# Two blocks in fp32 on one core: new places for the expert stage's inner values, the scatter and the modulation chunks

## Chip, cores, metric

One NeuronCore of a Trainium2 chip runs the whole program in one launch. The metric is the device time of that launch in microseconds (us), lower is better.

## What is computed

x is 256 tokens by 1024 features, everything in fp32. A first block of two layers (windowed attention and MLP, then an RG-LRU block and MLP), then a second block: three mixers side by side, and a mixture of experts. The parts around the change are:

```python
def sq_relu_mlp(h, w1, w2):                      # D_FF = 4096
    return jnp.square(jax.nn.relu(h @ w1)) @ w2

def ada_modulation_2(cond, w, b):                # once for c, once for c_ctx
    return jnp.split(jax.nn.silu(cond) @ w + b, N_MOD, axis=-1)

hx = modulate(rmsnorm(x, norm1_g[layer]), mod_x[0], mod_x[1])
hc = modulate(rmsnorm(ctx, norm1_g[layer]), mod_c[0], mod_c[1])

for e in range(N_EXPERTS):                       # 16 experts, each token belongs to one group of 4
    he = (jax.nn.silu(h @ w_gate[e]) * (h @ w_up[e])) @ w_down[e]
    out = out + combine[:, e:e + 1] * he.astype(jnp.float32)
x = x + mod_x[5] * ff_x.reshape(B, L, D)
return rmsnorm(x, final_norm_g)
```

## The kernel before

**Stream of pieces.** All weights come in pieces of 128 partitions x 1024 fp32 (512 KB) through a ring of six buffers (RING, in load_program, lines 350 to 381). SyncE issues the DMA of a piece when the one six places earlier in the stream has been used up. A "w" piece is a weight for TensorE. An "a" piece is a modulation chunk's half: VectorE multiplies it with a condition vector and sums along the row (modulation, L1307), which gives a column of the modulation table MOD.

**Split of a weight.** TensorE multiplies fp32 as three products of rounded halves (mm3). ScalarE writes a piece's high part w_high (high_upto, L911), VectorE subtracts it and writes the low part w_low (low_upto, L1299). Both have four slots, so ScalarE may write the high part of a piece only when TensorE is through with the piece four places earlier (the wait on `used`). VectorE waits for w_high, TensorE for w_low. Every engine executes its list in order; VectorE's instructions are all issued through one helper, so the profile gives them line L347, and nearly all matmuls line L388: one goes by tile names.

**Second MLP of the first block** (W_MLP1, turns 8 to 15; mlp at L517, L995 and L1476). A turn handles 512 hidden features with eight w pieces, four for the first product (X0 to X3) and four for the second (S4 to S7), of 24 matmuls each. On VectorE the splits of a turn are those of S4 to S7, called L4 to L7 here, and those of the next turn's X0 to X3, L8 to L11. Between them stand the inner values (r_two, the square, and h_low, its low part, for halves a = 0 and 1) and two chunks of modulation, of two pieces each. The first 8 chunks of ada_w_2 are "double": each piece is multiplied with two condition vectors (c and c_ctx), which is two instructions on the tile junk instead of one. Before, turns 8 to 11 take the 8 double chunks and turns 12 to 15 take 8 single ones. Between turn 11 and turn 12 the context ctx is normalised and modulated (rms_rows, modulate_norm), and its low part is made.

**Experts** (L827 to L900 on TensorE, L1214 to L1247 on ScalarE, L1869 to L1910 on VectorE). The 256 tokens are sorted by group into tiles of 128 slots. Experts 0 to 3 work on two tiles, experts 4 to 15 on one. The order of pieces in the stream (MOE_SEQ, L78) for step p is: the gate pieces of expert p+1 (G0 to G3), the down pieces of expert p (D0 to D3), and the up pieces of expert p+1 (U0 to U3). For one tile each piece is six matmuls of 128x512. In step p TensorE does

```python
        if p < NE - 1:
            gate(p + 1, 0, 1)
        turn(p)
        if p < NE - 1:
            gate(p + 1, 1, 4)
        down(p)
        if p < NE - 1:
            up(p + 1)
        if p % 4 == 3:
            scatter(p // 4)
```

where turn(p) is four transposes of the expert's hidden values he (L856). The inner values of an expert are: ScalarE's sigmoid of the gate product (signs, tile sge), VectorE's product of the two (gates, tile sge), VectorE's he = sge * weight * up product (products, L1874, which waits for U3 of that expert), TensorE's transposes, ScalarE's high part (he_high) and VectorE's low part (turned, he_low). VectorE has the twelve splits of step p, called L0 to L11 (L0 is G0's, L4 is D0's, L8 is U0's). Before, the list reads: L0 to L3, products(p), L4, turned(p), L5 to L7, gates(p+1), L8 to L11.

**Results.** After four experts, the sum of a group lies in PSUM. ScalarE copies it out (results, L1224, tile y_experts). TensorE multiplies it with a 0/1 matrix that puts the rows back to their tokens (scatter, L873), in four rounds r through two banks, and VectorE adds each round to x with the modulation factor (results, L1884, add_branch). TensorE's round r waits for VectorE's additions of round r-2.

Of the kernel before, what the change touches and what calls it, by code (L numbers as in the profile page):

```python
# [26 lines left out]
D, S, P = 1024, 256, 128  # L27
# [43 lines left out]

ADA_COL = [2 * j for j in range(48)] + [96 + 2 * j for j in range(24)]

# [67 lines left out]
def y_at(i):  # L141

    return 0 if i == 0 else i % 2
# [239 lines left out]
def tensor_program(nc, m, s, arrived):  # L383
# [455 lines left out]
    def gate(p, first, last):  # L839
        if first == 0 and p > 0:  # L840
            pe.wait_ge(s.silu, tiles_upto(p - 1))
        for n in range(first, last):
            hidden(p, "g", n)

    def up(p):
# [26 lines left out]

    def scatter(i):  # L873

        tiles = tiles_of(4 * i)
        pe.wait_ge(s.y_out, i + 2)
        for r in range(4):
            if r >= 2 or i > 0:
                pe.wait_ge(s.x_add, X_MOE + 8 * i + 2 * (r - 2) + 2)
            for d in (2 * r, 2 * r + 1):  # L880
                for a, tile in enumerate(tiles):
                    ins = mm(PS[:, 1 + 2 * (r % 2), (d % 2) * 256:(d % 2 + 1) * 256], m.YE[:, y_at(i) + a, d * P:(d + 1) * P], m.SCAT[:, tile, :], a == 0, a == len(tiles) - 1)
            ins.then_inc(s.sc_mm, 1)

# [3 lines left out]
    for p in range(NE):  # L888
# [5 lines that stand above are left out]
        down(p)  # L894
        if p < NE - 1:
            up(p + 1)
        if p % 4 == 3:
            scatter(p // 4)
    square_sums(SQ_END, m.MEAN, m.T2, KT)


def scalar_program(nc, m, s, arrived, cvec, par, rpar, xT, tab, ident_d, gw, ctxT, posT, tab2, fpar, moe_tab):
# [175 lines left out]
    act.wait_ge(s.in_late, 48)  # L1078
    rms_rows(m.CTX, KT, m.T2, D, 4, None)
    modulated(MOD_CTX, 1)  # L1080
    mlp(W_MLP1 + 32, 12, 4)
    layer_norm(3)
# [154 lines left out]
    for p in range(NE):  # L1237
        w = MOE_AT.get((p + 1, "g", 0), W_END)
        high_upto(w + 5)
        turned(p)  # L1240
        if p < NE - 1:
            high_upto(w + 8)
            signs(p + 1)
            high_upto(w + 12)
        if p % 4 == 3:
            results(p // 4)
    rms_rows(m.X, KT, m.T2, D, 10, (s.x_add, X_MOE + 26, 2), m.MEAN)  # L1247

# [44 lines left out]
def vector_program(nc, m, s, arrived):  # L1293
# [12 lines left out]

    def modulation(junk, conds=((0, 0),), only=range(2)):  # L1307

        for j in only:
            c = ADA_AT[2 * ada[0] + j]  # L1310
            vv.wait_ge(arrived[c % RING], 16 * (c // RING + 1))
            for n, (v, off) in enumerate(conds):
                col = ADA_COL[ada[0]] + off + j
                op(vv.tensor_tensor_reduce, junk, m.piece(c), m.CB[:, v, :], 1.0, 0.0, ALU.mult, ALU.add, m.MOD[:, col:col + 1],
                   inc=s.ada if n == len(conds) - 1 else None)
        ada[0] += 1

# [157 lines left out]

    def mlp(w0, t0, turns, conds=((0, 0),)):  # L1476
        for i in range(turns):
            t, w = t0 + i, w0 + 8 * i
            low_upto(w + 5)
            for a in range(2):  # L1480
                vv.wait_ge(s.relu, 2 * t + a + 1)
                if t >= 1:
                    vv.wait_ge(s.h_high, 2 * t + a - 1)
                op(vv.tensor_tensor, m.R2[:, a, :], m.R1[:, a, :], m.R1[:, a, :], ALU.mult, inc=s.relu2)
                vv.wait_ge(s.h_high, 2 * t + a + 1)
                op(vv.tensor_tensor, m.H1[1][:, a, :], m.R2[:, a, :], m.H1[0][:, a, :].bitcast(F32), ALU.subtract, inc=s.h_low)
                if a == 0:
                    low_upto(w + 6)
                    modulation(m.junk_mlp, conds)
                    low_upto(w + 7)  # L1490
            low_upto(w + 8)
            modulation(m.junk_mlp, conds)
            low_upto(w + 12)
# [63 lines left out]
    vv.wait_ge(s.silu_cc, 1)  # L1557
    mlp(W_MLP1, 8, 4, ((1, 0), (0, 48)))
    vv.wait_ge(s.in_late, 48)
    bias(144, 16, "ada_b2", 0)  # L1560
    rms_rows(4, m.CTX, m.CTX)
    lows = modulate_norm(MOD_CTX, m.CTX, "n1g", 144, 152, 1)
    lows()
    mlp(W_MLP1 + 32, 12, 4, ((1, 0),))
    op(vv.tensor_scalar, m.gate1, m.MOD[:, 88:96], 1.0, None, ALU.add)
# [317 lines left out]

    def results(i):  # L1884
        for r in range(4):
            vv.wait_ge(s.sc_mm, 4 * i + r + 1)
            for d in (2 * r, 2 * r + 1):
                add_branch(d, PS[:, 1 + 2 * (r % 2), (d % 2) * 256:(d % 2 + 1) * 256], m.MOD[:, 136 + d:137 + d])

# [7 lines left out]
    for p in range(NE):  # L1897
        w = MOE_AT.get((p + 1, "g", 0), W_END)
        if p > 0:
            low_upto(w + 4)  # L1900
            products(p)
            if p % 4 == 0:
                results(p // 4 - 1)
        low_upto(w + 5)
        turned(p)
        if p < NE - 1:
            low_upto(w + 8)
            gates(p + 1)
            low_upto(w + 12)
    results(3)  # L1910
    rms_rows(10, m.X[:, :, :], m.T1[:, :, :])
# [174 lines left out]
```

## Time and profile before

| | us |
|---|---|
| Median of 3 runs | 1676.21 (1666.42 to 1679.6) |
| Profiled execution, its own time | 1678.0 |
| Its span, first to last instruction | 1676.7 |
| TensorE (PE) busy | 1376.2 (82%) |
| VectorE (DVE) busy | 1159.0 (69%) |
| ScalarE (ACT) busy | 719.8 (43%) |
| Mean DMA rate over the span | 186 GB/s |

Times in a row of the trace are in us from the span's start. In a timeline row the bracket says how long the engine had been idle before the row, and what ended that. "PE" is TensorE's matmuls, whose ends are modelled, so that neighbouring matmuls overlap in the rows: the pace is the distance of their starts. PEclk in a table of windows is the granted TensorE clock, as a share of full speed.

### The profile page before, as it was taken

What the parts mean: (1) busy time and instruction counts of PE and PEld (TensorE: products, weight loads), DVE (VectorE), ACT (ScalarE), POOL (GpSimd) and SP (SyncE); (2) the same over time, 40 slices, a digit from 0 to 9 for tenths busy, and PEclk for the clock granted to TensorE, in tenths of its full rate; (3) what the DMA queues carried; (4) which work ended last, traced back from release to release, by engine and by line L of the source; (5) the groups of instructions that cost most, each with busy time, mean ns of one, the idle gap of its engine ahead of it and who ended that gap; (6) DMA issues with size and microseconds to landing.
All of it is one profiled execution on the core that took longest, in us unless ns stands there. A gap on an engine that the chain in (4) does not pass through costs nothing.

```text
span 1676.7 us, 20860 instructions
## 1 busy us (share of the span) xinstructions
PE 1376.2 (82%) x7808; PEld 1200.5 (72%) x7808; DVE 1159.0 (69%) x1541; ACT 719.8 (43%) x896; POOL 63.1 (4%) x54
## 2 busy tenths in 40 slices
PE   0862799997999977888985998655789999888885
PEld 0752799996777756888974797544777777777674
DVE  6657677776577567788766656985465557777775
ACT  2332335442565663334432333111244445666663
POOL 1100010000000001000000000430000000000000
PEclk9985999999999988999987998886889999999998
DMA  8425487874566445665760463100054556878782
GB/s 350 151 75 213 151 258 277 286 260 145 201 235 219 163 145 210 227 218 184 273 217 20 144 208 126 39 0 10 1 204 146 179 178 220 298 263 299 269 300 77
DMA packets 84069, 311.90 MB, mean 186 GB/s; under 512 B 9344, under 2 KB 9568, under 8 KB 83360
## 3 DMA queue, kind: packets, MB, share of 16 engines
q1 hardware_dynamic: 82080, 298.88, 51.1%
q10 hardware_dynamic: 1888, 11.69, 2.1%
q8 instruction: 61, 1.00, 0.2%
q14 instruction: 40, 0.33, 0.1%
HBM read 309.48 MB, written 1.05 MB: 185 GB/s over the span
## 4 chain that ended last, share of the span: by engine, by line
PE 61%; DVE 29%; ACT 6%; issue 2%; DMA 2%; DVEq 0%; POOL 0%; ACTq 0%; SPq 0%; POOLq 0%
PE ps L388 60%; DVE w_low L347 10%; DVE junk L347 5%; ACT w_high L347 2%; DVE t_one L347 1%; DVE t_two L347 1%; DVE rs L347 1%; DVE he L347 1%; DVE qp L347 1%; DMA ring<-stream 1%; DVE x L347 1%; PE ps L856 1%; DMA ring<-moe 1%; DVE sc L347 1%; DVE pf L347 1%
## 5 line engine op out<-in xcount | busy, mean ns | idle before, releaser
L347 DVE TENSOR_TENSOR w_low<-ring,w_high 128x1024 fp32r<-128x1024 f32 x376 | 461.6, 1228 | 196.2 <-ACT w_high L347 170.4
L347 ACT ACTIVATE w_high<-ring 128x1024 fp32r<-128x1024 f32 x376 | 398.9, 1061 | 327.1 <-PE ps L388 276.3
L388 PE MATMUL ps<-x_high,w_high 128*128 128x256 f32 (+1 forms) x784 | 235.8, 301 | 79.2 <-DVE x_low L347 71.6
L388 PE MATMUL ps<-x_low,w_high 128*128 128x256 f32 (+1 forms) x784 | 233.0, 297 | 0.0
L388 PE MATMUL ps<-x_high,w_low 128*128 128x256 f32 (+1 forms) x784 | 232.7, 297 | 0.0
L388 PEld LDWEIGHTS ps<-x_high,w_high 128*128 128x128 f32 x784 | 154.5, 197 | 90.5 <-issue 84.2
L347 DVE CUSTOM_DVE_ANT_0 junk<-ring,cond 128x1024 f32<-128x1024 f32 x133 | 165.3, 1243 | 20.9 <-DMA ring<-stream 3.6
L388 PE MATMUL ps<-h_high,w_high 128*128 128x256 f32 x512 | 147.7, 289 | 10.9 <-DVE h_low L347 10.9
L388 PEld LDWEIGHTS ps<-x_high,w_low 128*128 128x128 f32 x784 | 154.5, 197 | 2.8
L388 PEld LDWEIGHTS ps<-x_low,w_high 128*128 128x128 f32 x784 | 154.7, 197 | 2.5
L388 PE MATMUL ps<-h_low,w_high 128*128 128x256 f32 x512 | 146.9, 287 | 0.0
L388 PE MATMUL ps<-h_high,w_low 128*128 128x256 f32 x512 | 146.9, 287 | 0.0
L388 PE MATMUL ps<-w_high,xg_high 128*128 128x512 f32 x320 | 133.4, 417 | 0.0
L388 PE MATMUL ps<-w_low,xg_high 128*128 128x512 f32 x320 | 129.5, 405 | 0.0
L388 PE MATMUL ps<-w_high,xg_low 128*128 128x512 f32 x320 | 128.6, 402 | 0.0
L388 PE MATMUL ps<-x_whole,ring 128*96 128x256 f32 x512 | 114.8, 383 | 5.9 <-DVE x_whole L347 5.9
L388 PEld LDWEIGHTS ps<-h_high,w_high 128*128 128x128 f32 x512 | 100.4, 196 | 12.1 <-DVE h_low L347 12.1
L388 PEld LDWEIGHTS ps<-x_whole,ring 128*96 128x96 f32 x512 | 84.4, 165 | 33.9 <-issue 6.2
L388 PEld LDWEIGHTS ps<-h_low,w_high 128*128 128x128 f32 x512 | 100.6, 196 | 0.0
L388 PEld LDWEIGHTS ps<-h_high,w_low 128*128 128x128 f32 x512 | 100.4, 196 | 0.0
L388 PEld LDWEIGHTS ps<-w_high,xg_low 128*128 128x128 f32 x320 | 63.2, 198 | 14.0
L388 PEld LDWEIGHTS ps<-w_high,xg_high 128*128 128x128 f32 x320 | 63.7, 199 | 13.2
(299 smaller groups left out, 2170.3 us busy)
## 6 DMA issues: line engine op xcount, KB each, us to landing
ring<-stream SPq DMA_DIRECT2D x376, 512.0 KB, 4.6
ring<-moe SPq DMA_DIRECT2D x192, 512.0 KB, 4.6
tab_two<-tab ACTq DMA_DIRECT2D x1, 2824.0 KB, 14.1
gw<-gw ACTq DMA_DIRECT2D x1, 2304.0 KB, 13.3
cond<-cvec ACTq DMA_DIRECT2D x3, 512.0 KB, 6.8
x<-xT ACTq DMA_DIRECT2D x1, 1024.0 KB, 12.0
ctx<-ctxT ACTq DMA_DIRECT2D x1, 1024.0 KB, 4.8
pos<-posT ACTq DMA_DIRECT2D x1, 1024.0 KB, 6.9
```

Source lines behind the costliest of these rows:

```text
L347: return op(*a, **k).then_inc(self.sem, 1)
L388: return pe.matmul(out, stationary, moving, start=start, stop=stop, skip_group_check=True)
L856: ins = pe.transpose(PS[:, 2 + a, k * P:(k + 1) * P], m.HE[:, a, k * P:(k + 1) * P], m.ident)
```

## The change

Three parts. (1) In the second expert loop, for p >= 4, products(p) and turned(p) are moved ahead of splits: VectorE does L0, products, L1, L2, turned, L3 to L5, gates, L6 to L11, and ScalarE's copies are placed to match. ScalarE's copy of a group's results (y_experts) now stands ahead of the last two high parts of its step, where it stood behind them. (2) The scatter of a group is no longer one block after up(p+1); its four rounds follow the four gate pieces of expert 5, 9 and 13, and VectorE's additions stand one round at a time between L2 and gates. The last group's scatter stays at the end. (3) The chunks of ada_w_2 are reordered so that double and single ones alternate (A2_ORDER), one piece of a turn's first chunk is moved behind h_low of a = 1, and the context's modulation is moved from behind turn 11 to behind turn 14. Its normalisation stays behind turn 11.

```diff
+A2_ORDER = [0, 8, 1, 9, 2, 10, 3, 11, 4, 12, 5, 13, 6, 7] + list(range(14, 24))
+ADA_COL = [2 * j for j in range(48)] + [96 + 2 * j for j in A2_ORDER]
@@ TensorE
         for n in range(first, last):
             hidden(p, "g", n)
+            if p >= 5 and p % 4 == 1:
+                scatter(p // 4 - 1, n)
@@
-    def scatter(i):
+    def scatter(i, r):
@@
-        if p % 4 == 3:
-            scatter(p // 4)
+    for r in range(4):
+        scatter(3, r)
@@ ScalarE
     rms_rows(m.CTX, KT, m.T2, D, 4, None)
+    mlp(W_MLP1 + 32, 12, 3)
     modulated(MOD_CTX, 1)
-    mlp(W_MLP1 + 32, 12, 4)
+    mlp(W_MLP1 + 56, 15, 1)
@@
-        high_upto(w + 5)
+        high_upto(w + (5 if p < 4 else 3))
         turned(p)
         if p < NE - 1:
-            high_upto(w + 8)
+            high_upto(w + (8 if p < 4 else 6))
             signs(p + 1)
-            high_upto(w + 12)
+            high_upto(w + 10)
         if p % 4 == 3:
             results(p // 4)
+        if p < 4:
+            high_upto(w + 12)
@@ VectorE, MLP
+    def conditions():
+
+        col = ADA_COL[ada[0]]
+        if col < 96:
+            return ((0, 0),)
+        return ((1, 0), (0, 48)) if col < 112 else ((1, 0),)
...
                 if a == 0:
                     low_upto(w + 6)
-                    modulation(m.junk_mlp, conds)
+                    modulation(m.junk_mlp, conditions(), (0,), False)
                     low_upto(w + 7)
+            modulation(m.junk_mlp, conditions(), (1,))
             low_upto(w + 8)
-            modulation(m.junk_mlp, conds)
+            modulation(m.junk_mlp, conditions())
             low_upto(w + 12)
@@
-    mlp(W_MLP1, 8, 4, ((1, 0), (0, 48)))
+    mlp(W_MLP1, 8, 4)
     vv.wait_ge(s.in_late, 48)
+    rms_rows(4, m.CTX, m.CTX)
+    mlp(W_MLP1 + 32, 12, 3)
     bias(144, 16, "ada_b2", 0)
-    rms_rows(4, m.CTX, m.CTX)
     lows = modulate_norm(MOD_CTX, m.CTX, "n1g", 144, 152, 1)
     lows()
-    mlp(W_MLP1 + 32, 12, 4, ((1, 0),))
+    mlp(W_MLP1 + 56, 15, 1)
@@ VectorE, experts
         if p > 0:
-            low_upto(w + 4)
+            low_upto(w + (4 if p < 4 else 1))
             products(p)
-            if p % 4 == 0:
-                results(p // 4 - 1)
-        low_upto(w + 5)
+        low_upto(w + (5 if p < 4 else 3))
         turned(p)
         if p < NE - 1:
-            low_upto(w + 8)
+            for r in range(4):
+                low_upto(w + 3 + r)
+                if p >= 4 and p % 4 == 0:
+                    results(p // 4 - 1, r)
+            if p < 4:
+                low_upto(w + 8)
             gates(p + 1)
-            low_upto(w + 12)
-    results(3)
+            if p < 4:
+                low_upto(w + 12)
+    for r in range(4):
+        results(3, r)
```

Place one: VectorE in the one-tile experts, steps without results, before. sge is gates, he is products, he_low is turned.

```order
L347 TENSOR_TENSOR sge_1024_148<-sge_1024_148,ps 128x512
L347 TENSOR_TENSOR w_low<-ring_6144_49,w_high 128x1024 x8
L347 SCALAR_TENSOR_TENSOR he_1024_149<-sge_1024_148,rout_1024_146,ps 128x512
L347 TENSOR_TENSOR w_low<-ring_6144_49,w_high 128x1024
L347 TENSOR_TENSOR he_low<-ps,he_high 128x512
L347 TENSOR_TENSOR w_low<-ring_6144_49,w_high 128x1024 x3
```

The same place of the change (the helper's line is now L349):

```order
L349 TENSOR_TENSOR sge_1024_148<-sge_1024_148,ps 128x512
L349 TENSOR_TENSOR w_low<-ring_6144_49,w_high 128x1024 x7
L349 SCALAR_TENSOR_TENSOR he_1024_149<-sge_1024_148,rout_1024_146,ps 128x512
L349 TENSOR_TENSOR w_low<-ring_6144_49,w_high 128x1024 x2
L349 TENSOR_TENSOR he_low<-ps,he_high 128x512
L349 TENSOR_TENSOR w_low<-ring_6144_49,w_high 128x1024 x3
```

The eight splits between gates and products were L8 to L11 and the next step's L0 to L3. Now they are seven, L6 to L11 and the next L0: gates stands two splits earlier, products three.

Place two: TensorE around the first scatter, before. y_experts and scat are the scatter, ident and he the transposes of expert 4.

```order
L388 MATMUL ps<-w_high,xg_low 128x512
L388 MATMUL ps<-scat_1280_145,y_experts_2048_153 128x256 x16
L388 MATMUL ps<-w_high,xg_high 128x512
L388 MATMUL ps<-w_low,xg_high 128x512
L388 MATMUL ps<-w_high,xg_low 128x512
L388 MATMUL ps<-w_high,xg_high 128x512
L388 MATMUL ps<-w_low,xg_high 128x512
L388 MATMUL ps<-w_high,xg_low 128x512
L856 MATMUL ps<-ident_128_59,he_1024_149 128x128 x4
```

The same place of the change:

```order
L390 MATMUL ps<-w_high,xg_low 128x512
L390 MATMUL ps<-scat_1280_145,y_experts_2048_153 128x256 x4
L860 MATMUL ps<-ident_128_59,he_1024_149 128x128 x4
L390 MATMUL ps<-w_high,xg_high 128x512
L390 MATMUL ps<-w_low,xg_high 128x512
L390 MATMUL ps<-w_high,xg_low 128x512
L390 MATMUL ps<-w_high,xg_high 128x512
L390 MATMUL ps<-w_low,xg_high 128x512
L390 MATMUL ps<-w_high,xg_low 128x512
L390 MATMUL ps<-scat_1280_145,y_experts_2048_153 128x256 x4
```

Sixteen matmuls in a row have become four groups of four, the first between gate piece G0 and the transposes, each later one behind a gate piece.

Place three: VectorE at the start of turn 8 of the second MLP, before. ISA rows on junk are the modulation products.

```order
L347 TENSOR_TENSOR w_low<-ring_6144_49,w_high 128x1024
L347 ISA junk_1024_70,mod_160_56<-ring_6144_49,cond_2048_55 128x1024
L347 ISA mod_160_56 128x1
L347 ISA junk_1024_70,mod_160_56<-ring_6144_49,cond_2048_55 128x1024
L347 ISA mod_160_56 128x1
L347 ISA junk_1024_70,mod_160_56<-ring_6144_49,cond_2048_55 128x1024
L347 ISA mod_160_56 128x1
L347 ISA junk_1024_70,mod_160_56<-ring_6144_49,cond_2048_55 128x1024
L347 ISA mod_160_56 128x1
L347 TENSOR_TENSOR w_low<-ring_6144_49,w_high 128x1024
L347 TENSOR_TENSOR r_two_1024_86<-r_one_1024_85 128x512
L347 TENSOR_TENSOR h_low<-r_two_1024_86,h_high 128x512
```

The same place of the change:

```order
L349 TENSOR_TENSOR w_low<-ring_6144_49,w_high 128x1024
L349 ISA junk_1024_70,mod_160_56<-ring_6144_49,cond_2048_55 128x1024
L349 ISA mod_160_56 128x1
L349 ISA junk_1024_70,mod_160_56<-ring_6144_49,cond_2048_55 128x1024
L349 ISA mod_160_56 128x1
L349 TENSOR_TENSOR w_low<-ring_6144_49,w_high 128x1024
L349 TENSOR_TENSOR r_two_1024_86<-r_one_1024_85 128x512
L349 TENSOR_TENSOR h_low<-r_two_1024_86,h_high 128x512
L349 ISA junk_1024_70,mod_160_56<-ring_6144_49,cond_2048_55 128x1024
L349 ISA mod_160_56 128x1
L349 ISA junk_1024_70,mod_160_56<-ring_6144_49,cond_2048_55 128x1024
```

Two of the four products between L5 and L6 now stand behind h_low of a = 1.

## Rows read from the trace of the kernel before

**Rows 1.** The page, part 1: busy us, share, instructions.

```profile
PE 1376.2 (82%) x7808; PEld 1200.5 (72%) x7808; DVE 1159.0 (69%) x1541; ACT 719.8 (43%) x896; POOL 63.1 (4%) x54
```

**Rows 2.** Windows: stretch, length, busy us, PEclk, DMA share, GB/s.

```profile
796.90:819.90 23.00, 23.00 (x194) 23.00 (x193) 17.50 (x20) 10.91 (x12) 0.00 (x0) 1.00 0.82 279
...
1402.00:1426.00 24.00, 21.91 (x98) 18.00 (x98) 19.21 (x21) 14.87 (x15) 0.00 (x0) 1.00 0.64 221
1426.00:1447.00 21.00, 18.60 (x76) 14.99 (x76) 16.71 (x16) 13.77 (x15) 0.00 (x0) 0.92 0.83 296
```

**Rows 3.** Timeline of one step of the one-tile experts, 1425 to 1448.

```profile
1427.08 0.66 PE L856 MATMUL ps<-ident,he 128*128 128x128 f32 x4 [2.72 <-DVE he L347]
...
1428.78 0.63 PE L388 MATMUL ps<-w_low,xg_high 128*128 128x512 f32 x1
1429.21 0.63 PE L388 MATMUL ps<-w_high,xg_low 128*128 128x512 f32 x1
...
1435.95 0.69 DVE L347 TENSOR_TENSOR sge<-sge,ps 128x512 f32<-128x512 f32 x1
...
1436.74 10.55 DVE L347 TENSOR_TENSOR w_low<-ring,w_high 128x1024 fp32r<-128x1024 f32 x8
...
1438.27 0.39 PE L388 MATMUL ps<-w_low,he_high 128*128 128x512 f32 x1
1438.49 0.39 PE L388 MATMUL ps<-w_high,he_low 128*128 128x512 f32 x1
```

**Rows 4.** The chain, in order of time: products of experts 4, 5, 8, 9, 12, 13, 15.

```profile
1400.54 0.76 DVE he L347
...
1426.28 0.76 DVE he L347
...
1489.84 0.76 DVE he L347
...
1515.75 0.76 DVE he L347
...
1577.70 0.76 DVE he L347
...
1604.37 0.76 DVE he L347
...
1646.49 0.76 DVE he L347
```

**Rows 5.** Timeline around the first scatter, 1390 to 1406.

```profile
1391.94 2.09 ACT L347 ACTIVATE y_experts<-ps 128x1024 f32<-128x1024 f32 x2
...
1401.39 2.11 DVE L347 SCALAR_TENSOR_TENSOR x<-ps,mod,x 128x256 f32<-128x256 f32 x4
1402.45 3.72 PE L388 MATMUL ps<-scat,y_experts 128*128 128x256 f32 x16 [2.86 <-DVE x L347]
```

**Rows 6.** DMA in the step 1426 to 1447: count, size, median landing.

```profile
ring<-moe SPq DMA_DIRECT2D x12, 512.0 KB, 5.3
```

**Rows 7.** DMA in the stretch 5 to 30, the fullest of the run.

```profile
DMA packets 2813, 10.13 MB, mean 405 GB/s; under 512 B 319, under 2 KB 447, under 8 KB 2685
...
ring<-stream SPq DMA_DIRECT2D x12, 512.0 KB, 6.3
```

**Rows 8.** Timeline of VectorE in the second MLP, 648 to 776.

```profile
648.86 1.23 DVE L347 TENSOR_TENSOR w_low<-ring,w_high 128x1024 fp32r<-128x1024 f32 x1 [3.43 <-ACT w_high L347]
...
682.75 1.23 DVE L347 CUSTOM_DVE_ANT_0 junk<-ring,cond 128x1024 f32<-128x1024 f32 x1
683.90 0.08 DVE L347 DVE_READ_ACCUMULATOR2_ANT mod<- 128x1 f32 x1
...
732.12 2.55 DVE L347 TENSOR_TENSOR w_low<-ring,w_high 128x1024 fp32r<-128x1024 f32 x2 [0.46 <-DVE w_low L347]
...
768.39 3.57 DVE L347 TENSOR_SCALAR t_two<-ctx,misc,mod 128x256 f32<-128x256 f32 x8
...
775.25 1.23 DVE L347 TENSOR_TENSOR w_low<-ring,w_high 128x1024 fp32r<-128x1024 f32 x1
```

More of the change, by code:

```diff
@@ L70 @@
 RNN_AT = {key: W_RNN + n for n, key in enumerate(RNN_SEQ)}
-ADA_COL = [2 * j for j in range(48)] + [96 + 2 * j for j in range(24)]
+A2_ORDER = [0, 8, 1, 9, 2, 10, 3, 11, 4, 12, 5, 13, 6, 7] + list(range(14, 24))
+ADA_COL = [2 * j for j in range(48)] + [96 + 2 * j for j in A2_ORDER]
 POOL_PIECES = (1, 6, 11)
@@ L871, in down @@
             ins.then_inc(s.used, 1)
-    def scatter(i):
+    def scatter(i, r):
         tiles = tiles_of(4 * i)
         pe.wait_ge(s.y_out, i + 2)
[L877 to L883, printed above, removed]
+        if r >= 2 or i > 0:
+            pe.wait_ge(s.x_add, X_MOE + 8 * i + 2 * (r - 2) + 2)
+        for d in (2 * r, 2 * r + 1):
+            for a, tile in enumerate(tiles):
+                ins = mm(PS[:, 1 + 2 * (r % 2), (d % 2) * 256:(d % 2 + 1) * 256], m.YE[:, y_at(i) + a, d * P:(d + 1) * P], m.SCAT[:, tile, :], a == 0, a == len(tiles) - 1)
+        ins.then_inc(s.sc_mm, 1)
     gate(0, 0, 4)
@@ L1305, in low_upto, with modulation @@
             low[0] += 1
-    def modulation(junk, conds=((0, 0),), only=range(2)):
+    def modulation(junk, conds=((0, 0),), only=range(2), last=True):
         for j in only:
@@ L1315, in modulation @@
                    inc=s.ada if n == len(conds) - 1 else None)
-        ada[0] += 1
+        if last:
+            ada[0] += 1
     def bias(a, n, name, j):
@@ L1474, in vector_program, with mlp @@
     project(W_ATT, m.gate1)
-    def mlp(w0, t0, turns, conds=((0, 0),)):
+    def conditions():
[3 more added lines that the diff above has]
+        return ((1, 0), (0, 48)) if col < 112 else ((1, 0),)
+    def mlp(w0, t0, turns):
         for i in range(turns):
@@ L1882, in turned, with results @@
             op(vv.tensor_tensor, m.HB[1][:, a, :, :], PS[:, 2 + a, :].rearrange("p (k s) -> p k s", k=4), m.HB[0][:, a, :, :].bitcast(F32), ALU.subtract, inc=s.e_low)
[L1884 to L1888, printed above, removed]
+    def results(i, r):
+        vv.wait_ge(s.sc_mm, 4 * i + r + 1)
+        for d in (2 * r, 2 * r + 1):
+            add_branch(d, PS[:, 1 + 2 * (r % 2), (d % 2) * 256:(d % 2 + 1) * 256], m.MOD[:, 136 + d:137 + d])
     low_upto(W_MOE + 8)
@@ L2030 @@
     a = [[ada(I["ada_w"][i, m]) for m in range(2)] for i in range(2)]
-    a2 = ada(I["ada_w_2"][0])
+    a2 = ada(I["ada_w_2"][0])[A2_ORDER]
     wi = I["attn_w_in"][0]
```

## The prediction

> **What bounds the kernel now.** I read the page first. TensorE is busy for 82% of the span and VectorE for 69% [rows 1], so neither is full on average and the answer lies in the stages. The windows come next [rows 2]: in the second MLP with single chunks TensorE is busy for all 23.00 us of a turn, at a granted clock of 1.00; in the one-tile experts it is busy for 18.60 of 21 us, at 0.92, and VectorE for 16.71. There nobody is full, so the step must be a loop of waits, and the timeline shows it [rows 3]. TensorE stands still for 2.72 us ahead of the transposes, since products is late. Products is late because VectorE first has eight splits in a row (10.55 us). The last of these, L3, needs a slot that comes free only when TensorE is through with U3: so a high part on ScalarE, a split and products lie between U3 and the transposes. After the stop the matmuls start 0.43 us apart instead of 0.22, the lower clock level. These slow gate pieces free the slots late, and the next run of splits starts late. Stop and slow stretch feed each other. The chain has one products per expert [rows 4]: 245.95 us from expert 4 (1400.54) to expert 15 (1646.49).
>
> **Experts, a plain step after the change.** Nothing is added or dropped; the instructions stand elsewhere. On VectorE there are 12 splits at 1.33 (10.55 for 8, with the gap behind), gates at 0.79 (1435.95 to 1436.74), turned at the same 0.79 (same shape, my choice) and products at 0.85 (1400.54 to 1401.39): 16.0 + 2.4 = 18.4 us [rows 3 to 5]. TensorE needs 72 matmuls at about 0.227, 1.36 us a piece, and 0.4 for the transposes (0.66 in their row, less the tail of the last): 16.7. Neither can give less than 18.4. Now the waits. Products waits for U3 of its expert only, 0.25 us after the last matmul; G0 (1.36 us) covers products (0.85), so the transposes no longer wait. Behind products stand L1, L2, turned, L3 to L5, gates and L6, and D2 needs L6: 0.85 + 2.66 + 0.79 + 3.99 + 0.79 + 1.30 = 10.4 us. From D2 to U3 TensorE is the slower one: 6 x 1.36 = 8.2. With 0.25 that makes 18.8 us. What hides in it: VectorE's 0.4 us of waiting for U3, and three stops of TensorE of about 0.7 us, ahead of G1, G3 and D2. I add 0.2 for pieces that land late: 19.0.
>
> **The DMA queue.** A step moves 12 x 0.524 = 6.3 MB. In 18.8 us that is 335 GB/s, where the window shows 296 [rows 2]. A piece is asked for when the split six places earlier ends, and ScalarE wants it one high part ahead of its own split (shape of a y_experts copy, 1.05 us [rows 5]). The tightest place of my step is the next G0: 5.6 us between the two; all others have 6.3 or more. Landing takes 5.3 us in a step now, and 6.3 when the queue is full, at 405 GB/s for 25 us on end [rows 6, 7]. So 335 fits, closely. The Trainium skill ("DMA: Bandwidth & Descriptors", Where 436 GB/s comes from) says that a load from HBM is held to about 358 GB/s per core. This trace does not agree: 405 GB/s over 25 us [rows 7]. By the page's figure the new step would fill 94% of the memory's rate and the queue would be the next bound, which is the second rival below.
>
> **Steps with a scatter** (into experts 5, 9, 13). The additions cost 8 x 0.53 = 4.2 us on VectorE (2.11 for four) [rows 5], and the later scatters 3.6 us on TensorE (8 matmul rows a pair of rounds at 0.23). Before, TensorE stood for 2.86 us within the scatter for the additions [rows 5]. Now each round has a gate piece or a split beside it. On the path stand 18.8 + 4.2 = 23.0. The first has two tiles, so 7.3 us of scatter: there round 1 delays the additions and I get 25. Before, the three took 25.74, 25.91 and 26.67 [rows 4]: 78.3 against 25.2 + 23.1 + 23.1 = 71.4.
>
> **The steps with ScalarE's copy** (7 to 8, 11 to 12). y_experts waits for D3 and takes 1.05 us (2.09 for two) [rows 5], and now stands ahead of the high parts of U2 and U3: L10 starts about 1.1 us late. So 20.1. **The last step** (14 to 15): products(15) stands behind all splits, ten in a row, as before: 18.4 + 3 x 1.33 = 22.4, say 22.5. **The start**: expert 4's products has L10, L11 and the next L0 ahead of it behind the two copies instead of four splits behind them. By the same counting products(4) comes 2.2 us earlier.
>
> Sum [rows 4]: experts 5 to 8 took 63.56, now 19 + 19 + 20.1 = 58.1, saved 5.5; 9 to 12 took 61.95, saved 3.8; 13 to 15 took 42.12, now 41.5, saved 0.6; scatter steps save 6.9; start 2.2. **Experts: -19.0 us.** Behind expert 15 nothing moves.
>
> **Second MLP.** A double turn costs VectorE 8 splits (10.6), 8 products of 1.23 + 0.08 and a small gap (11.0), the four inner values (3.0, at the 0.69 of sge's shape [rows 3] and gaps); the rest to 28.2, 3.6 us, are waits on ScalarE within the inner values. The three turns from 648.86 to 733.45 (the second split of the row at 732.12) took 28.2 each [rows 8]. A turn with one double and one single chunk has two products fewer (2.75), and one of the waits, which I put at 0.5, is covered, as a product now stands where VectorE waited for L7's high part: 24.9, taken as 24.8. TensorE's bound is 23.0 [rows 2]. So turns 8 to 10 save 3.3 each; turn 11 saves 3.0 up to its last matmul; turns 12 and 13 lose 24.8 - 23.0 = 1.8 each; turn 14, all double, is 27.5 and loses 4.5. That is +12.9 - 8.1 = 4.8 saved. The context's modulation (768.39 to 775.25, 6.9 us with its low parts [rows 8]) stops VectorE once either way: bounds +1.5 and -1.5, I take 0. The first MLP has 1.00 and a full TensorE with single chunks; VectorE is busy for only 17.5 of 23 us in such a turn [rows 2], which hides a moved product: 0. If that cover were gone it would cost 1.3 us a turn. **MLP: -4.8 us.**
>
> In all 19.0 + 4.8 = 24 us. The profiled execution took 1678.0 for a span of 1676.7, 1.8 us over the median of 1676.2; the difference carries over: 1652.
>
> **Rivals.** (a) *Forecast.* (b) *The DMA queue becomes the bound.* If landing rises to the 6.3 us of a full queue [rows 7], the next G0 comes 0.7 us late, and the run behind it a little more: some 1.1 us in each of 11 steps, 12 us: 1664. For it: the DMA share is 0.83 at 296 GB/s [rows 2], which by proportion is 357 at 1.00. Against: 405 in rows 7. (c) *The low clock stays.* If each expert still has eight matmuls at 0.43 instead of 0.22, 1.6 us in 8 steps comes back: 13 us, 1665. For it: TensorE still stops three times. Against: stops of 0.7, not 2.7; and in the window with the stop of 2.86 the clock was 1.00 [rows 2, 5]. (d) *Slower.* The short stops could hold TensorE at the low level for most of a step. A piece then takes 2.56 us instead of 1.36. Five such pieces of twelve cost 6.0 x 11 = 66 us: 1718. It decides from 24 / 11 = 2.2 us a step, nearly two pieces, and is slower by over 1% from three and a half. Now two pieces a step are slow after a stop four times as long [rows 3], so I give it little. (e) *The MLP gives nothing*, the doubles of turn 14 and the context's modulation eating the gain: 1657. (f) *It does not do what it says* has no ground: the orders show each move.
>
> **How the numbers follow.** Chances: (a) 0.73, (b) 0.10, (c) 0.06, (d) 0.04, (e) 0.07. A measurement of this kernel tells about 1% from no change, which is 1659.4. (a) spans 1641 to 1660: its lower end is VectorE full at 18.4 and no late piece (7 us less) and runs 4 us apart. I count 0.71 of it and (e) as faster, (b), (c) and the rest of (a) as same. The range 1640 to 1665 takes in (b), (c) and (e).
>
> **What would show it.** Right: products every 19 us in the plain steps and 23 in the later scatter steps; no stop above 1 us ahead of the transposes; PEclk 1.00 in the one-tile experts and about 330 GB/s; turns of 24.8 us in the second MLP at 8 to 13 and 27.5 at 14. Wrong: ScalarE's high parts waiting for DMA more than 1 us a step (b), matmuls 0.43 apart (c, d), or turns 12 and 13 above 26 us (e).

## The result and the profile after

The changed kernel takes 1655.8 us, the median of 9 runs (1652.17 to 1657.51), against 1676.21 of 9 runs before: a ratio of 0.9893, 95% interval 0.9869 to 0.9917 (the two medians alone give 0.9878, the two means 0.9897). The profiled execution took 1654.29 (span 1653.0), 23.7 us less than the profiled one of before, 1678.0. The runs of the kernel before lie in two groups, four at 1666.4 to 1667.0 and five at 1676.2 to 1679.6; what parts them is looked at in the last section.

The page, part 1, of the changed kernel: TensorE is busy for 12.3 us less [rows 1] with the same 7808 matmuls, so part of the gain is clock.

```profile
PE 1363.9 (83%) x7808; PEld 1182.8 (72%) x7808; DVE 1159.7 (70%) x1541; ACT 719.7 (44%) x896; POOL 63.4 (4%) x54
```

Windows of the changed kernel (stretch, length, busy us of PE, PEld, DVE, ACT, POOL, then PEclk, DMA share, GB/s): a plain one-tile step, a scatter step, and two turns of the second MLP.

```profile
1418.00:1437.00 19.00, 17.84 (x78) 13.82 (x77) 16.92 (x16) 13.23 (x15) 0.00 (x0) 1.00 0.95 328
1476.00:1499.00 23.00, 20.66 (x92) 16.43 (x91) 20.39 (x23) 13.65 (x15) 0.00 (x0) 1.00 0.77 265
757.20:782.00 24.80, 23.48 (x194) 23.10 (x193) 19.96 (x24) 10.94 (x12) 0.00 (x0) 1.00 0.55 194
782.00:806.80 24.80, 23.48 (x194) 23.10 (x193) 19.98 (x24) 10.91 (x12) 0.00 (x0) 1.00 0.69 253
```

PEclk is 1.00 where it was 0.92 [rows 2], and the queue moves 328 GB/s instead of 296 (322 to 337 in the five plain steps). The timeline of one plain step of the changed kernel shows why:

```profile
1436.76 0.75 DVE L349 SCALAR_TENSOR_TENSOR he<-sge,rout,ps 128x512 f32<-128x512 f32 x1 [0.61 <-PE ps L390]
...
1437.92 0.60 PE L860 MATMUL ps<-ident,he 128*128 128x128 f32 x4
...
1438.89 0.50 PE L390 MATMUL ps<-w_high,xg_high 128*128 128x512 f32 x1 [0.37 <-DVE w_low L349]
...
1442.35 0.50 PE L390 MATMUL ps<-w_high,xg_high 128*128 128x512 f32 x1 [0.42 <-DVE w_low L349]
...
1445.85 9.21 DVE L349 TENSOR_TENSOR w_low<-ring,w_high 128x1024 fp32r<-128x1024 f32 x7
...
1447.13 0.50 PE L390 MATMUL ps<-w_high,he_high 128*128 128x512 f32 x1 [0.36 <-DVE w_low L349]
```

The 2.72 us ahead of the transposes [rows 3] are gone: products (he) now waits for TensorE, 0.61 us, and not the other way round. Three short stops are left, ahead of G1, G3 and D2, each a bracket of some 0.4 us and a longer first matmul, about 0.7 us in all. Seven splits stand in a row where eight did.

The chain of the changed kernel, products of experts 5, 6, 8, 9, 12, 13, 14 and 15:

```profile
1417.85 0.76 DVE he L349
...
1436.76 0.76 DVE he L349
...
1475.69 0.76 DVE he L349
...
1499.05 0.76 DVE he L349
...
1556.97 0.76 DVE he L349
...
1580.32 0.76 DVE he L349
...
1599.24 0.76 DVE he L349
...
1621.63 0.76 DVE he L349
```

A plain step takes 18.9 us instead of 21.1 (1417.85 to 1436.76), the second and third scatter step 23.4 (1475.69 to 1499.05, 1556.97 to 1580.32) instead of 25.9 and 26.7, the last 22.4. The first scatter step begins at 1393.24 and takes 24.6 instead of 25.7. From the timeline of the changed kernel, products of expert 4 and the first round of the first scatter, which lies behind G0 and waits for nothing. This scatter has two tiles, so a round is eight matmuls; the sixteen matmuls and the groups of four shown under place two are those of the later scatters.

```profile
1393.24 0.75 DVE L349 SCALAR_TENSOR_TENSOR he<-sge,rout,ps 128x512 f32<-128x512 f32 x1 [0.51 <-PE ps L390]
...
1394.43 1.89 PE L390 MATMUL ps<-scat,y_experts 128*128 128x256 f32 x8
```

The DMA of the window 1418 to 1437, and what ScalarE waited for from 1400 to 1622 (us in total, times, longest):

```profile
ring<-moe SPq DMA_DIRECT2D x12, 512.0 KB, 5.4
```

```profile
ACT w_high L349 <- DMA ring<-moe: 12.1, 21, 1.2
```

Landing is 5.4 us, and ScalarE's waits for pieces come to 1.1 us a step. The plain steps still take 18.9 us, where 18.8 was counted without late pieces, so the waits lengthen them by little.

In the second MLP the alternating turns take 24.8 us, but between turn 11 and turn 12 (the context's normalisation) ScalarE and VectorE of the changed kernel stand:

```profile
742.32 1.06 ACT L349 ACTIVATE w_high<-ring 128x1024 fp32r<-128x1024 f32 x1 [4.84 <-DMA ring<-stream]
743.70 1.06 ACT L349 ACTIVATE w_high<-ring 128x1024 fp32r<-128x1024 f32 x1 [0.33 <-DMA ring<-stream]
745.26 1.06 ACT L349 ACTIVATE w_high<-ring 128x1024 fp32r<-128x1024 f32 x1 [0.50 <-DMA ring<-stream]
746.41 2.62 ACT L349 ACTIVATE t_two<-ctx 128x512 f32<-128x512 f32 x4
747.09 5.23 PE L390 MATMUL ps<-t_two,ones 128*128 128x256 f32 x16 [4.07 <-ACT t_two L349]
...
752.92 1.75 DVE L349 RECIPROCAL rs<-rs 128x256 f32<-128x256 f32 x1 [5.01 <-ACT rs L349]
```

The squares stand behind ScalarE's high parts of the next turn's pieces, and these wait for their transfers. TensorE has nothing to do for 4.07 us, and then does the sixteen matmuls of the squares in 5.23 us, 0.33 each.

Stage by stage, the profiled execution after against the one before: second MLP up to the first addition to x (863.07) -3.1; the stages between it and products of expert 3, which the change does not touch, -2.2; experts from there up to products of expert 15 -19.9; behind it +1.2; ahead of the second MLP +0.3. Sum -23.7.

### The profile page after: what moved, and what is told of

Its sections match the earlier page's. It is cut to its first block, busy times and chain, and to the rows that moved or that the text cites. A ratio compares the mean times of both kernels' runs of the same rounds, so it can differ in the third digit from the quotient of the medians.

```text
span 1653.0 us, 20870 instructions
## 1 busy us (share of the span) xinstructions
PE 1363.9 (83%) x7808; PEld 1182.8 (72%) x7808; DVE 1159.7 (70%) x1541; ACT 719.7 (44%) x896; POOL 63.4 (4%) x54
## 4 chain that ended last, share of the span: by engine, by line
PE 61%; DVE 29%; ACT 6%; issue 2%; DMA 1%; DVEq 0%; POOL 0%; ACTq 0%; SPq 0%; POOLq 0%
PE ps L390 60%; DVE w_low L349 8%; DVE junk L349 6%; ACT w_high L349 2%; DVE t_one L349 1%; DVE t_two L349 1%; DVE x L349 1%; DMA ring<-stream 1%; DVE rs L349 1%; DVE he L349 1%; DVE r_two L349 1%; DVE qp L349 1%; DVE pf L349 1%; ACT h_high L349 1%; DVE sc L349 1%
## 5 line engine op out<-in xcount | busy, mean ns | idle before, releaser
L349 DVE TENSOR_TENSOR w_low<-ring,w_high 128x1024 fp32r<-128x1024 f32 x376 | 461.7, 1228 | 167.1 <-ACT w_high L349 138.1
L349 ACT ACTIVATE w_high<-ring 128x1024 fp32r<-128x1024 f32 x376 | 398.8, 1061 | 303.6 <-PE ps L390 173.9
L349 DVE CUSTOM_DVE_ANT_0 junk<-ring,cond 128x1024 f32<-128x1024 f32 x133 | 165.9, 1247 | 20.5 <-DMA ring<-stream 2.6
L390 PE MATMUL ps<-w_high,xg_high 128*128 128x512 f32 x320 | 129.7, 405 | 9.9 <-DVE w_low L349 9.9
L390 PE MATMUL ps<-w_low,xg_high 128*128 128x512 f32 x320 | 125.3, 391 | 0.0
L390 PE MATMUL ps<-w_high,xg_low 128*128 128x512 f32 x320 | 125.2, 391 | 0.0
L390 PE MATMUL ps<-w_high,he_high 128*128 128x512 f32 x160 | 65.7, 411 | 9.6 <-DVE w_low L349 8.1
```

Source lines behind the costliest of these rows:

```text
L349: return op(*a, **k).then_inc(self.sem, 1)
L390: return pe.matmul(out, stationary, moving, start=start, stop=stop, skip_group_check=True)
```

## The experiments

All ratios are to the kernel before, with their 95% interval. The kernel before was run beside each of them, on the same chip; the experiments themselves are spread over three chips. Unless said otherwise a cut shows the difference to the changed kernel, and `...` marks lines left out.

**One part of the change alone.** The expert part (VectorE, ScalarE and scatter), second MLP as before:

```diff
-A2_ORDER = [0, 8, 1, 9, 2, 10, 3, 11, 4, 12, 5, 13, 6, 7] + list(range(14, 24))
+A2_ORDER = list(range(24))
...
-    mlp(W_MLP1 + 32, 12, 3)
     modulated(MOD_CTX, 1)
-    mlp(W_MLP1 + 56, 15, 1)
+    mlp(W_MLP1 + 32, 12, 4)
...
```

> The change with its MLP part undone (chunks in their old order, both pieces of a chunk together, the context's modulation behind turn 11). Theory (the stop for products and the slow matmuls behind it feed each other, and the new order removes both): plain one-tile steps at 18.9 us and a clock of 1.00 as in the change; expert 4 to 15 in 228 to 230 us; about 20 us less than before in the profile, ratio near 0.988. Rival (the experts gain less alone, and the rest came with the MLP part): less than 15 us.

Measured: 1654.56 us, 0.9877 (0.9836 to 0.9918). Plain steps 18.9, scatter steps 24.6, 23.3 and 23.4, from expert 4 to 15 229.1 us. Its interval covers that of the whole change: what the MLP part adds to it can't be told from nothing here.

The second MLP's part alone, experts as before:

> Before with the MLP part alone. Theory: from the split L4 of turn 8 to the first addition to x 214 us instead of 217, everything behind as before, plain expert steps still 21.1 us at clock 0.92; 3 us less in all, which is a ratio of 0.998 and not to be told from 1. Rival: the earlier arrival moves the clock's or the DMA's phase in the stages behind, and more than 5 us go or come outside the MLP.

Measured: 1674.85, 0.9991 (0.9974 to 1.0007). The turns are 24.8 us as in the changed kernel, the experts 246.1 as before, and the time is that of before. The MLP part gave nothing that these runs can tell from zero; the interval holds the 3 us expected as well.

**The two halves of the expert part**, both with the second MLP as before. The spread scatter without the moved inner values:

```diff
         if p > 0:
-            low_upto(w + (4 if p < 4 else 1))
+            low_upto(w + 4)
             products(p)
-        low_upto(w + (5 if p < 4 else 3))
+        low_upto(w + 5)
         turned(p)
...
```

> Before with the scatter's rounds spread over the gate pieces alone; the inner values stay at their old places. Theory: the stop of 2.86 us for the additions goes in three steps, plain steps stay at 21.1 us with the stop ahead of the transposes and clock 0.92; 4 to 8 us less in all. Rival (the scatter block is what makes the expert stage slow): more than 12 us less.

Measured: 1667.97, 0.9923 (0.9887 to 0.9959); experts 4 to 15 238.7 us, 7.3 less than before. The runs show 9.8 us less by the medians, more than the 4 to 8 expected, and one plain step of 19.5 was not expected either; it is shown below. The moved inner values with the scatter in one piece as before:

> Before with the inner values moved alone; the scatter is one block behind the up pieces again, with all additions behind products. Theory: plain steps at 18.9 us and clock 1.00, scatter steps at 25 us or more because TensorE still stands for the additions; 12 to 16 us less in all. Rival (the scatter block decides): under 8 us less.

Measured: 1659.74, 0.9902 (0.9868 to 0.9937); experts 4 to 15 230.6, 15.4 less than before; both halves together gave 16.8 in the kernel with the expert part alone. The halves do not add up: with products early, the second and third scatter step take 23.4 us with the scatter in one piece too, and only the first differs (26.1 against 24.6). So the scatter's place on TensorE does not set these two; a plain step and the 4.2 us of additions on VectorE make 23.1.

The windows of two neighbouring plain steps of the scatter-only kernel, and the transposes that begin them, show what else a step's length hangs on:

```profile
1423.08:1442.57 19.49, 17.00 (x76) 13.83 (x76) 16.82 (x15) 13.94 (x14) 0.00 (x0) 1.00 0.90 304
1442.57:1463.70 21.13, 18.63 (x76) 15.10 (x76) 16.84 (x15) 13.94 (x14) 0.00 (x0) 0.92 0.86 317
```

```profile
1423.88 0.66 PE L860 MATMUL ps<-ident,he 128*128 128x128 f32 x4 [1.95 <-DVE he L349]
...
1443.38 1.00 PE L860 MATMUL ps<-ident,he 128*128 128x128 f32 x4 [2.50 <-DVE he L349]
1444.03 0.78 PE L390 MATMUL ps<-w_high,xg_high 128*128 128x512 f32 x1
1444.61 0.63 PE L390 MATMUL ps<-w_low,xg_high 128*128 128x512 f32 x1
1445.03 0.63 PE L390 MATMUL ps<-w_high,xg_low 128*128 128x512 f32 x1
```

Same instructions, same order. After the stop of 1.95 us the granted clock stays at 1.00 (2.4 GHz) and the step takes 19.5 us; after 2.50 us it falls (0.92 over the step), the matmuls start 0.42 us apart, and the step takes 21.1. The stops are not what makes the difference themselves: all but their last 0.8 us, in both cases, lie ahead of products and so outside the step that is measured.

**The stop filled, nothing else changed.** Kernel before (the cut is against it), with eleven matmuls more on TensorE, whose output nothing reads, ahead of the transposes of eight experts:

```diff
         if p < NE - 1:
             gate(p + 1, 0, 1)
+            if p >= 5 and p % 4:
+                for _ in range(11):
+                    mm(PS[:, 1, :], m.XGH[:, 0, 0:P], m.XGL[:, 0, 0:512], True, True)
         turn(p)
```

> Before, with eleven extra matmuls of 128x512 (2.5 us, into a bank nobody reads) between the first gate piece and the transposes of experts 5 to 7, 9 to 11, 13 and 14, so that TensorE works through its stop; they add work and change no result. Theory (the low clock behind the stop is a cost of its own): clock 1.00 in these steps, matmuls 0.23 us apart behind the transposes, and plain steps fall from 21.1 to between 19.3 and 20.3 us although products stands where it did. Rival (the slow matmuls are covered by VectorE's run of splits): still 21 us or more.

Measured: 1667.13, 0.993 (0.9899 to 0.9961). From the timeline and the windows of this kernel:

```profile
1424.60 2.65 PE L388 MATMUL ps<-xg_low,xg_high 128*128 128x512 f32 x11
1427.51 0.33 PE L856 MATMUL ps<-ident,he 128*128 128x128 f32 x1 [0.26 <-DVE he L347]
```

```profile
1426.71:1446.22 19.51, 19.25 (x88) 15.68 (x87) 16.83 (x15) 13.96 (x14) 0.00 (x0) 1.00 0.90 310
```

The transposes come no earlier; yet the plain steps fall from 21.1 to 19.5 us, and experts 4 to 15 from 245.95 to 236.1. Of the 2.2 us that the change takes off a plain step, 1.6 are the price of the low clock behind the stop, and 0.6 are left for the order itself. The stop does not need the slow matmuls: with them gone TensorE would still stand for about 2.9 us (2.65 filled and 0.26), where it stood for 2.72.

**Products late again.** Changed kernel, but products of the one-tile experts behind L3 and turned behind it:

```diff
-            low_upto(w + (4 if p < 4 else 1))
+            low_upto(w + 4)
             products(p)
-        low_upto(w + (5 if p < 4 else 3))
+        low_upto(w + (5 if p < 4 else 4))
         turned(p)
...
```

> The change with products (and with it turned and ScalarE's he_high) put back behind the split of the fourth gate piece, in the one-tile experts; gates, scatter and MLP stay as in the change. Theory: products waits again for a slot that U3 frees, a high part and a split; a stop of 2 to 3 us ahead of the transposes is back, the matmuls behind it are 0.43 us apart, and plain steps take 20.5 to 21.5 us. Rival (the place of gates and the spread scatter carry the gain): plain steps stay below 19.5 us.

Measured: 1683.59, 1.0041 (1.0008 to 1.0074): slower than before. Its timeline:

```profile
1426.83 1.12 PE L860 MATMUL ps<-ident,he 128*128 128x128 f32 x4 [2.96 <-DVE he L349]
...
1434.70 13.19 DVE L349 TENSOR_TENSOR w_low<-ring,w_high 128x1024 fp32r<-128x1024 f32 x10 [0.49 <-ACT w_high L349]
```

Ten splits run between gates and products where before had eight, since gates stand earlier here; the stop is back (2.96 us) and three of the plain steps take 22.0 to 22.3 us at a granted clock of 0.92, longer than the 20.5 to 21.5 expected, and two take 20.9 at 1.00. So the late products cost 2.0 us a step with the full clock too. The place of products carries the gain; the earlier gates without it are a loss.

**The second chunk's place.** Changed kernel, with the second piece of the first chunk again between L5 and L6, beside the first:

```diff
-                    modulation(m.junk_mlp, conditions(), (0,), False)
+                    modulation(m.junk_mlp, conditions())
                     low_upto(w + 7)
-            modulation(m.junk_mlp, conditions(), (1,))
```

> The change with both pieces of a turn's first chunk between L5 and L6 again; the chunks still alternate. Theory: VectorE waits about 0.5 us a turn again ahead of L7, so alternating turns take 25.2 to 25.4 us instead of 24.8, and L7 comes 2 us earlier against the turn's start only in so far as the products do not delay h_low; the first MLP stays at 23.0 us a turn. Rival: TensorE's wait for h_low of half 1 comes back with its 1.8 us, and turns take over 26 us.

Measured: 1659.19, 0.9917 (0.9886 to 0.9948). Turns 8 and 9 take 26.6 us and turn 10 25.2, instead of 24.8 (their inner values stand at 650.39, 677.01 and 703.63), and the first addition to x comes at 868.18 instead of 863.07. TensorE's stop of turn 8 for h_low, and the windows of turns 8 and 10:

```profile
663.08 0.39 PE L390 MATMUL ps<-h_high,w_high 128*128 128x256 f32 x1 [1.83 <-DVE h_low L349]
```

```profile
650.39:677.01 26.62, 24.79 (x194) 24.59 (x193) 19.98 (x25) 10.93 (x12) 0.00 (x0) 0.94 0.81 289
703.63:728.85 25.22, 23.39 (x194) 23.14 (x193) 19.98 (x25) 10.95 (x12) 0.00 (x0) 1.00 0.68 230
```

All three turns have the stop of 1.83 us, which is 0.28 in the changed kernel. Over the 5 us behind it the granted clock is 0.66 in turns 8 and 9 and 1.00 in turn 10. Where the clock holds, the turn takes the 25.2 of the theory; where it falls, 26.6, over the rival's 26. So the alternation alone brings the turn from 27.75 to 25.2, and the moved piece the last 0.4 and, in two turns of three, the 1.4 of slow matmuls behind the stop that it removes.

**The context's squares early.** Changed kernel, with the squares on ScalarE ahead of turn 11:

```diff
-    mlp(W_MLP1, 8, 4)
+    mlp(W_MLP1, 8, 3)
     act.wait_ge(s.in_late, 48)
-    rms_rows(m.CTX, KT, m.T2, D, 4, None)
+    for k in range(0, KT, 2):
+        A(m.T2[:, k:k + 2, :], m.CTX[:, k:k + 2, :], ACT.Square, s.sq)
+    mlp(W_MLP1 + 24, 11, 1)
+    root(4, m.RSTD, m.VAR, 1.0 / D, "eps6")
     mlp(W_MLP1 + 32, 12, 3)
```

> The change with ScalarE's squares of the context ahead of turn 11 instead of behind its last high part. Theory (in the change the piece of the next turn's X3 lands late, since its place in the ring comes free with the later L7, and the squares stood behind its high part): TensorE's square sums start right behind the turn's last matmul and the context's reciprocal comes 3 to 4 us earlier, and all behind it. Rival: TensorE's next turn then waits for its own pieces, and less than 1 us is won.

Measured: 1649.23, 0.9857 (0.9756 to 0.9958), with two runs only and so a wide interval. The kernel was run again beside the changed kernel itself:

> The changed kernel once more, beside the three kernels below on the same chip. About 1655, ratio 0.987 to 0.991; products every 18.9 us in the plain steps; normalisation of the context with its reciprocal near 752.9 and the squares slow (over 5 us). It is the level from which the next three are read.

> The changed kernel with the context's squares ahead of turn 11 on ScalarE, measured beside the changed kernel itself. Theory (the late squares, and the low clock behind the stop that they cause, ate the gain of turn 11): 4 to 6 us less than the changed kernel, reciprocal of the context near 748, squares 3.7 us on TensorE. Rival (the first measurement was a lucky draw of the clock): within 2 us of it.

Measured: the changed kernel 1654.91 (1652.61 to 1656.86, 6 runs), 0.9884 (0.9853 to 0.9915); with early squares 1648.71 (1644.29 to 1649.76, 6 runs), 0.9844 (0.9813 to 0.9875). Every run of the second lies below every run of the first; the medians are 6.2 us apart. From the timeline of the second:

```profile
742.18 1.06 ACT L349 ACTIVATE w_high<-ring 128x1024 fp32r<-128x1024 f32 x1 [4.86 <-DMA ring<-stream]
...
742.70 2.54 PE L390 MATMUL ps<-t_two,ones 128*128 128x256 f32 x11
...
748.02 1.75 DVE L349 RECIPROCAL rs<-rs 128x256 f32<-128x256 f32 x1
```

ScalarE waits for its piece as long as in the changed kernel, 4.86 us, but TensorE has the squares' matmuls right behind its own (0.23 us each), and the reciprocal stands at 748.0 instead of 752.9 and 752.5 in the two profiled executions of the changed kernel. From the inner values of turn 8 that is 98.5 us instead of 101.6 and 102.7.

**The last expert.** The kernel with early squares, and products(15) three splits earlier on VectorE, turned(15) one split ahead of the end on VectorE and ScalarE:

```diff
-            low_upto(w + (4 if p < 4 else 1))
+            low_upto(W_END - 3 if p == NE - 1 else w + (4 if p < 4 else 1))
             products(p)
-        low_upto(w + (5 if p < 4 else 3))
+        low_upto(W_END - 1 if p == NE - 1 else w + (5 if p < 4 else 3))
         turned(p)
+        low_upto(W_END if p == NE - 1 else 0)
...
```

> Changed kernel, the context's squares ahead of turn 11 on ScalarE, and expert 15's products three splits earlier on VectorE, its turned values one split ahead of the end. Theory (the last step is long only because ten splits stand ahead of products): step 14 to 15 falls from 22.4 to 18.9 or so, the stop of TensorE ahead of the last transposes from about 3.5 to under 1.5 us, and the end comes 3 to 4.5 us earlier than in the kernel with early squares alone. Rival (the last down pieces wait for their splits anyway): the end moves by under 1 us.

Measured: 1645.5 (1641.77 to 1647.11, 6 runs), 0.9823 (0.9791 to 0.9854). The step from 14 to 15 takes 18.9 us instead of 22.4, and the last reciprocal stands at 1635.1 instead of 1637.9. From its timeline:

```profile
1613.89 0.66 PE L860 MATMUL ps<-ident,he 128*128 128x128 f32 x4 [0.84 <-DVE he L349]
1617.43 0.77 PE L390 MATMUL ps<-w_high,he_high 128*128 128x512 f32 x1 [2.89 <-DVE he_low L349]
```

The stop ahead of the transposes has gone from 4.3 to 0.84 us, and the one ahead of the first down matmul has grown from 1.50 to 2.89: he_low waits behind two splits on VectorE. From products of expert 14 to the last reciprocal the trace shows 3.0 us less (40.9 instead of 43.9), the medians 3.2: the lower edge of the 3 to 4.5 expected, and far from the rival's under 1.

The same expert part with the second MLP as before:

> Expert part of the change with the earlier products of expert 15, and the second MLP as before. If the MLP part of the change is worth nothing as it stands and little with early squares, this lies within 4 us of the kernel with everything; if alternating turns with early squares are worth the 4.8 that I forecast, it is 5 us slower than that.

Measured: 1656.0, 0.9873 (0.9836 to 0.991), but in two groups: 1645.9 and 1647.7, and four runs of 1655.7 to 1657.6. So the MLP part with early squares is worth 10.5 us by the medians and 8.7 by the means of six, more than the 4.8 forecast, and 1.3 against the mean of the two short runs. Neither answer foreseen fits; the last section has what the two groups share.

## Why the prediction was right, point by point

The forecast was 1652 with a range of 1640 to 1665 and 0.78 for faster by over 1%; 1655.8 lies in the range, and the ratio of 0.9893 is beyond 1%, though its interval reaches to 0.9917, so that part is likely and not certain. The sum was made against the profiled execution, 1678.0 - 24, and the profiled execution after is 23.7 shorter. That the two agree so closely is partly luck: the second MLP gave 1.7 us less than forecast and the end cost 1.2 that I had at nothing, while 2.2 came from stages that the change does not touch, and 0.9 more than forecast from the experts. The 3.8 us between 1652 and 1655.8 lie mostly in the step to the median: I took the 1.8 us by which the profiled execution of before lay above its median as carrying over; the one of after lies 1.5 below its own.

- **A plain step of 19.0**: 18.9 to 19.0, in all five. The counting (0.85 + 9.55 from products to D2, then six pieces of TensorE) holds, as do the three stops. What I did not price apart: most of the old stop's cost was the clock behind it, 1.6 of 2.2, as the filled stop shows. The sum has both in it, since it counted the new step from full-speed matmuls. And "stop and slow stretch feed each other" holds one way only: the stop makes the slow stretch, but stays, at some 2.9 us, when the slow stretch is gone.
- **Scatter steps 25.2, 23.1, 23.1**: 24.6, 23.4, 23.4, together 71.3 against 71.4. But I tied the gain to the stop within the scatter (2.86 us in the first, 3.59 in the second); the halves show that for the later two steps the moved products alone do it.
- **Steps with ScalarE's copy 20.1**: 20.0 both. **Last step 22.5**: 22.4, and the ten splits ahead of products are its cause, as their removal shows. **Start 2.2 earlier**: 2.4 (from products of expert 3, 1366.94 to 1393.24, against 1371.87 to 1400.54).
- **Experts -19.0**: -19.9 up to products(15). "Behind expert 15 nothing moves" was wrong by 1.2 us, most of it ahead of the last scatter: from products of expert 15 to the last scatter 13.0 us pass instead of 11.9, at a granted clock of 0.65 instead of 0.71. The stop ahead of the last transposes has grown from 3.86 to 4.32 us, but that is not enough of a reason: the kernel with the inner values alone has a stop of 4.33 there and passes the stretch in 11.9 at 0.71. Why the clock stays low for longer is open.
- **The DMA queue**: 322 to 337 GB/s in the five plain steps against the 335 worked out, landing 5.4. Rival (b) falls, since the steps take 18.9. Its sign, ScalarE's waits for pieces above 1 us a step, did show (1.1), but hidden. The Trainium skill ("DMA: Bandwidth & Descriptors", Where 436 GB/s comes from) puts a core's HBM loads at about 358 GB/s; 337 as the mean of a step does not reach that, so this case still has only the 405 of [rows 7] against it.
- **Rivals (c) and (d)**: PEclk is 1.00 in all plain steps; three stops of about 0.7 us a step were followed by no fall of the clock.
- **Second MLP -4.8**: this term failed. In the profiled executions it is -3.1; the MLP part alone gave a ratio of 0.9991, so the total of rival (e) describes the MLP best, though not its reasons: turns 12 and 13 take 24.8, not above 26, and it is turn 11 that falls short. By the steps of the sum: the alternating turn (24.8) and the losses of turns 12 to 14 with the neutral modulation of the context (-8.1; from the reciprocal to the first addition to x 110.15 against 101.95, 8.2 more) are right. The double turn of before is 27.75, not 28.2: my three turns had one with a stretch of low clock in them. "Turn 11 saves 3.0 up to its last matmul" is the step that failed, or rather what it left out, the squares behind it: from the inner values of turn 11 to the reciprocal 27.0 us pass instead of 28.1, 1.0 saved. With both chunks shorter, TensorE ends turn 11 ahead of the squares on ScalarE, stands 4.07 us and does them at the lower clock. From the inner values of turn 8 to the reciprocal the change saves 11.3 us (101.55 against 112.8) where I had 12.9 and, against the expert part alone, in whose execution turn 10 and the squares lost nothing to the clock (108.6), only 7.0, less than the 8.2 that turns 12 to 14 lose. With the squares early, the same stretch takes 98.5.

## What to carry to other kernels

Where an instruction that others wait for is late because a run of splits stands ahead of it, move it up to the place where its own inputs are ready, and count the runs on both sides of it: with gates moved and products left in place, eight splits in a row became ten and the kernel slower. A stop of TensorE costs itself and, in many of the cases here from 1.83 us up, slow matmuls behind it; to price those, fill the stop with matmuls whose output nothing reads and look at the difference. And shortening a turn pays only if what follows it on the other engines is there in time: look at the next wait, not at the turn.

## What the runs showed of the hardware

The same code falls to the lower clock level in one execution and not in another. The second MLP is the same in the kernel with the expert part alone and in the one with the last expert added. Timeline of TensorE in the first, and then in the second, the start of the second product of turn 11 and the squares of the context:

```profile
747.21 0.39 PE L390 MATMUL ps<-h_high,w_high 128*128 128x256 f32 x1 [1.83 <-DVE h_low L349]
...
755.15 3.72 PE L390 MATMUL ps<-t_two,ones 128*128 128x256 f32 x16 [1.92 <-ACT t_two L349]
```

```profile
748.34 0.39 PE L390 MATMUL ps<-h_high,w_high 128*128 128x256 f32 x1 [1.83 <-DVE h_low L349]
...
757.77 2.66 PE L390 MATMUL ps<-t_two,ones 128*128 128x256 f32 x8 [1.92 <-ACT t_two L349]
```

Both stand 1.83 us and then 1.92 us. In the first the granted clock stays at 1.00 and a square takes 0.23 us; in the second it is 0.85 over the stretch from 746.3 to 757.8 and the first eight take 0.33 each. From the inner values of turn 8 to the reciprocal the first needs 108.6 us, the second 112.8, as the profiled execution of before. The layer norm behind the MLP does the same: from the first addition to x to its reciprocal it takes 12.1 to 12.4 us in six of the profiled executions and 14.8 to 15.2 in the other eight, with the same instructions. At products of expert 4, up to which the two kernels are the same code, these two executions are 8.5 us apart (1389.75 and 1398.25). The two ran on different chips, but the kernel before shows both of its groups on each of the three chips of the experiments.

That is nearly the size of the gap between the groups of runs of the kernel before (1667 and 1677) and of the one with the last expert moved and the old second MLP. All six kernels with the second MLP as before part into two such groups, whose means lie 7 to 12 us apart. Their six profiled executions agree with it: the two that belong to a lower group took 108.6 us for the stretch to the reciprocal and 12.1 for the layer norm, the four of an upper group 112.8 and 14.8. So the groups go with what the clock did in these two places; only one execution of each of them is profiled, and that nothing else adds to the gap is not shown. The layer norm alone parts nothing: the two profiled executions of the changed kernel took 15.1 and 12.3 us for it, and came out at 1654.3 and 1654.9. The kernels with the changed second MLP do not part: but for the one with late products (1673.8 to 1687.2) the runs of each lie within 6 us. That holds with the squares late, behind a stop of over 4 us, and with the squares early. Against a lower group the changed second MLP as it stands gains nothing (211.7 us from the inner values of turn 8 to the first addition to x, 210.8 in the expert part alone); against an upper group it gains 3.1.

What tips a stop one way or the other stays open. The stops of 0.7 us in the plain steps were never followed by a fall of the clock; 1.83 was in one execution and not in another, and in two turns of three within one execution (the piece put back, above); 1.95 was not, 2.50 was, and so were 3.59 within the second scatter of before (eight matmuls in 3.09 us instead of 1.89) and 4.07 ahead of the squares. But 2.86 within the first scatter of before [rows 5] was not [rows 2], nor was this one in the kernel with late products, whose step has a granted clock of 1.00:

```profile
1540.68 0.66 PE L860 MATMUL ps<-ident,he 128*128 128x128 f32 x4 [3.13 <-DVE he L349]
```

```profile
1539.88:1560.75 20.87, 17.44 (x76) 13.66 (x76) 16.84 (x16) 13.93 (x14) 0.00 (x0) 1.00 0.84 299
```

The Trainium skill ("TensorE: Matmul & The Clock Gate", What's actually happening) says of the slow matmuls at a kernel's start that their number differs from run to run, by the phase in which the gate happens to be. The pair of executions above shows such a difference from run to run in the middle of a kernel; whether the phase makes it, no run here can show.
